# 4 MB weight transfers from expert 8 on, the last two experts summed in PSUM, and the last norm's weight spread from one row, in a single-core MoE decoder step

## The reference, cut to what matters

```python
logits = (x2d @ router_w + router_b); top_val, top_idx = lax.top_k(logits, 4); gate = softmax(top_val)
# for each of 32 experts e, on the tokens that chose it:
u = xblk @ w_up[e] + b_up[e]                   # w_up[e]: 1024 x 2048, 8 MB
glu, lin = jnp.split(u, 2, axis=-1)            # clamp both at 7
act = glu * sigmoid(1.702 * glu) * (lin + 1.0)
y = act @ w_down[e] + b_down[e]                # w_down[e]: 1024 x 1024, 4 MB
x = x + g2 * (sum over experts of gate * y)
y_prompt, y_sample = rms_norm(x, final_norm_g) # the last norm, one weight row of 1024
```

## Time and profile before

| | us |
|---|---|
| median of three runs | 1158.92 |
| the profiled execution's own time | 1159.39 |
| its span, first to last instruction | 1157.6 |
| TensorE busy | 1112.3 (96%) |
| VectorE busy | 411.7 (36%) |
| ScalarE busy | 191.3 (17%) |
| GpSimd busy | 20.7 (2%) |

### The profile page before, as it was taken

How to read it: one execution, slowest core, us unless ns; L and a number is a source line. 1 busy time by engine, 2 the same in 40 slices (tenths; PEclk the granted TensorE clock), 3 DMA queues, 4 the chain that set the end, 5 groups by cost and what they waited for, 6 DMA issues and landing times.

```text
span 1157.6 us, 14316 instructions
## 1 busy us (share of the span) xinstructions
PE 1112.3 (96%) x5674; PEld 497.2 (43%) x5674; DVE 411.7 (36%) x841; ACT 191.3 (17%) x387; POOL 20.7 (2%) x53
## 2 busy tenths in 40 slices
PE   7999999999999999999999998999999999999996
PEld 5777778843333333333333333333333333333332
DVE  3145644353333333333333334333333333333334
ACT  2161223321111111111111111111111111111112
POOL 0101010000000000000000000000000000000001
PEclk9999999999999999999999998999999999999998
DMA  9987986989999999999999999999999999999995
GB/s 352 411 308 257 367 274 231 415 316 400 429 412 430 429 426 427 429 428 428 429 429 429 429 429 427 428 427 427 427 430 425 428 428 429 428 429 428 428 429 199
DMA packets 43323, 460.96 MB, mean 398 GB/s; under 512 B 6965, under 2 KB 7937, under 8 KB 13673
## 3 DMA queue, kind: packets, MB, share of 16 engines
q1 hardware_dynamic: 37072, 449.66, 93.2%
q0 software_dynamic: 2688, 9.47, 2.3%
q10 hardware_dynamic: 3512, 1.14, 0.4%
HBM read 455.60 MB, written 4.65 MB: 398 GB/s over the span
## 4 chain that ended last, share of the span: by engine, by line
PE 73%; DMA 25%; DVE 1%; ACT 1%; issue 0%; SPq 0%; DVEq 0%; ACTq 0%
PE bank L1431 27%; DMA ring<-in_w_up 20%; PE bank L1486 14%; PE bank L1091 9%; PE bank L1472 5%; PE bank L1402 4%; DMA ring<-in_w_down 3%; PE bank L1314 2%; PE bank L1449 2%; DMA ring<-in_w_ada 2%; PE bank L1036 1%; PE bank L1411 1%; PE bank L1195 1%; PE bank L1460 1%; PE bank L1172 1%; PE bank L1277 1%
## 5 line engine op out<-in xcount | busy, mean ns | idle before, releaser
L1431 PE MATMUL bank<-ring,arena 128*64 128x512 f32 x2016 | 448.6, 595 | 21.2 <-DMA ring<-in_w_up 21.2
L1431 PEld LDWEIGHTS bank<-ring,arena 128*64 128x64 f32 x2016 | 139.7, 137 | 320.2 <-issue 277.0
L1486 PE MATMUL bank<-ring,arena 128*64 128x512 f32 x992 | 220.1, 595 | 1.9 <-DMA ring<-in_w_down 1.9
L1486 PEld LDWEIGHTS bank<-ring,arena 128*64 128x64 f32 x992 | 68.6, 137 | 131.8 <-issue 129.0
L1091 PE MATMUL bank<-arena,ring 128*128 128x264 f32 x448 | 105.4, 390 | 0.8 <-DVE arena L1696 0.8
L2043 DVE COPY arena<-bank 128x512 f32<-128x512 f32 x32 | 22.1, 692 | 197.9 <-PE bank L1431 197.9
L890 ACT ACTIVATE arena<-bank 128x512 f32<-128x512 f32 x32 | 19.1, 598 | 442.1 <-PE bank L1431 442.1
L1091 PEld LDWEIGHTS bank<-arena,ring 128*128 128x128 f32 x448 | 83.1, 190 | 17.9 <-issue 4.5
L2097 DVE TENSOR_TENSOR arena<-bank,arena 128x512 f32<-128x512 f32 x32 | 22.1, 692 | 189.7 <-PE bank L1486 189.7
L2092 DVE TENSOR_TENSOR arena<-arena,bank 128x512 f32<-128x512 f32 x128 | 79.1, 680 | 5.4 <-PE bank L1472 5.4
L1472 PE MATMUL bank<-arena,gpickT 64*128 64x512 f32 x248 | 78.6, 628 | 0.0
(11 more groups left out here) (335 smaller groups left out, 688.4 us busy)
## 6 DMA issues: line engine op xcount, KB each, us to landing
ring<-in_w_up SPq DMA_DIRECT2D x125, 2048.0 KB, 29.1
ring<-in_w_down SPq DMA_DIRECT2D x61, 2048.0 KB, 28.1
ring<-in_w_ada SPq DMA_DIRECT2D x24, 1024.0 KB, 9.5
ring<-in_w_in SPq DMA_DIRECT2D x14, 1024.0 KB, 12.0
ring<-in_w_o SPq DMA_DIRECT2D x4, 1024.0 KB, 8.5
arena<-in_w_up SPq DMA_DIRECT2D x5, 512.0 KB, 18.8
arena<-in_w_down SPq DMA_DIRECT2D x5, 512.0 KB, 12.8
ring<-in_state_hgrn POOLq DMA_DIRECT2D x4, 512.0 KB, 13.3
```

What stands on the lines that cost most here:

```text
L1431: last = mm(bank[64 * half:64 * half + 64, b, :], xe[:, par, k % 4, k // 4, :], src[:, 512 * half:512 * half + 512], start=(k == 0), stop= ...
L1486: last = mm(bank[64 * half:64 * half + 64, b, :], acts[:, k, :], src[:, 512 * half:512 * half + 512], start=(k == 0), stop=(k == KT - 1))
```

## The change

1. **4 MB transfers.** `w_up` and `w_down` are laid out anew before the launch, so that the rows of two neighbouring loads lie side by side for each partition (`up_blocks`, `down_blocks`): 32 KB contiguous per partition. From load 52 to load 187 (body 8 to the up weights of expert 31) SP sends two loads with one DMA of 4 MB into two neighbouring slots. It waits for the second of the two old loads in them, and TensorE waits for the first slot's semaphore alone. These are 68 transfers in place of 136. Loads before 52 keep 2 MB (their 16 KB rows now lie 32 KB apart), and so do the last four, the down weights of 30 and 31. `PEEL` is 8, since the loop's bodies must all be of one kind.
2. **Last two experts in the banks.** `sums_to_banks` puts `acc` into the four PSUM banks with four identity matmuls, and the combines of 30 and 31 add onto them there. VectorE's eight last additions go, and the final norm reads the banks.
3. **The norm's weight.** SP sends one 4 KB row in body 16. TensorE multiplies it with a row of ones into two banks, and ScalarE makes four copies from these. TensorE waits for the copies (`rows_sb` 7) before it goes on. The three DMAs at the end go.
4. **Squares.** VectorE now squares the second quarter (a copy and an operation) and the sample rows. ScalarE squares the other three quarters and no longer the sample rows.

```diff
-PEEL, UNROLL = 4, 4
+PEEL, UNROLL = 8, 4
+PAIRED_FROM = UPS + PEEL * LOADS
+PAIRED_TO = LOADS * NE - 4
+def comes_with_last(i):
+    return PAIRED_FROM <= i < PAIRED_TO and i % 2 == 1
...
+                sp.dma_start(pairs[:, slot:slot + n, :].rearrange("p s n -> p (s n)"), src.rearrange("e p n -> p (e n)")
+                             ).then_inc(sem(f"pair{slot}"), 16)
...
-                    reuse(i, q)
+                    if comes_with_last(i):
+                        continue
+                    n = 2 if comes_with_last(i + 1) else 1
+                    reuse(i + n - 1, q)
...
+                if e0 == MIDDLE_AT:
+                    sp.wait_ge(sem("down_done"), 3)
+                    sp.dma_start(fgraw, a["final_norm_g"].unsqueeze(0)).then_inc(sem("fg_in"), 16)
...
-            sp.wait_ge(sem("up_done"), NE)
-            sp.dma_start(fgrow, a["final_norm_g"].unsqueeze(0).to_broadcast([P, D])).then_inc(sem("fg_in"), 16)
...
+                for half in range(2):
+                    act.wait_ge(sem("bias_psum"), half + 6)
+                    own, b = slice(64 * half, 64 * half + 64), (4, 7)[half]
+                    act.activation(fgrow[:, 512 * half:512 * half + 512], bank[:, b, :], ACT.Copy).then_inc(sem("rows_sb"), 1)
+                    act.activation(fgs[own, :], bank[own, b, :], ACT.Copy).then_inc(sem("rows_sb"), 1)
...
-            for m in range(3):
-                square(m)
-            act.wait_ge(sem("sums_ready"), 2)
+            for m in (0, 2, 3):
+                act.wait_ge(sem("acc_psum"), NA * (NE - 1) + m + 1)
+                od.did(A(ring[:, 14, 512 * m:512 * m + 512], bank[:, LAST_BANKS[m], :], ACT.Square,
                          accum_out=sumsq[:, m:m + 1]), sem("squares_ready"))
+            act.wait_ge(sem("sums_ready"), 4)
...
+            def sums_to_banks(stop):
+                for m, ((i, half), b) in enumerate(zip(COMBINE, LAST_BANKS)):
+                    last = mm(bank[:, b, :], ident[:, :], acc[i][:, 512 * half:512 * half + 512], start=True, stop=stop)
...
+                pe.wait_ge(sem("fg_in"), 16)
+                for half in range(2):
+                    mm(bank[:, (4, 7)[half], :], ones[0:1, :], fgraw[:, 512 * half:512 * half + 512], start=True, stop=True
+                       ).then_inc(sem("bias_psum"), 1)
+                pe.wait_ge(sem("rows_sb"), 7)
...
             down(NE - 2, ld, rd)
+            sums_to_banks(False)
             down(NE - 1, ld, rd, (0,), 3, actT_last)
-            combine(NE - 2, LAST_BANKS, NE, None, NE)
+            combine(NE - 2, LAST_BANKS, NE, None, NE, start=False, stop=False)
             down(NE - 1, ld, rd, (1,), 3, actT_last)
-            pe.wait_ge(sem("acc_used"), NA * (NE - 1))
-            combine(NE - 1, LAST_BANKS, NE, None, NE, gpickT_last)
+            combine(NE - 1, LAST_BANKS, NE, None, NE, gpickT_last, start=False)
...
-            add_up(NE - 2, LAST_BANKS)
+            dve.wait_ge(sem("acc_psum"), NA * (NE - 1))
-            add_up(NE - 1, LAST_BANKS)
...
+            v.tensor_copy(ring[:, 15, 0:512], bank[:, LAST_BANKS[1], :]).then_inc(sem("sums_ready"), 1)
+            STT(ring[:, 15, 512:D], ring[:, 15, 0:512], 1.0, bank[:, LAST_BANKS[1], :], ALU.mult, ALU.mult,
+                accum_out=sumsq[:, 1:2]).then_inc(sem("sums_ready"), 1)
+            STT(junk_s, ys, 1.0, ys, ALU.mult, ALU.mult, accum_out=sumsq_s[:, 0:1]).then_inc(sem("sums_ready"), 1)
...
+def up_blocks(w):
+    return w[0].reshape(NE, 2, 2, P, 2, 2 * D).transpose(0, 1, 3, 2, 4, 5).reshape(NE, 2, P, 8 * D)
+def down_blocks(w):
+    return w[0].reshape(NE, 2, P, 4, D).transpose(0, 2, 1, 3, 4).reshape(NE, P, 8 * D)
```

More of the change, by code:

```diff
@@ L540, in body @@
                     else:
-                        load(i, e + 1 if kind == "up" else e, kind, k)
+                        load(i, e + 1 if kind == "up" else e, kind, k, n)
             load_aside(ASIDES[1], (0, 1, 2))
@@ L550, in _ @@
                 i = last_load(e, kind, k)
-                reuse(i)
-                load(i, e, kind, k)
+                if comes_with_last(i):
+                    continue
+                n = 2 if comes_with_last(i + 1) else 1
+                reuse(i + n - 1)
+                load(i, e, kind, k, n)
             i = last_load(*LAST[-1])
@@ L1417, in up @@
                     slot = loads(s)
[L1418 to L1421 removed]
+                    if rounds(s) is not None:
+                        pe.wait_ge(sem("aside_in" if slot < 0 else f"pair{slot}"), rounds(s))
                     if s == parts:
@@ L1461, in gates, with combine @@
                 last.then_inc(sem("gpick_psum"), 1)
-            def combine(n, banks, xes, sampled=None, picks=None, gT=gpickT):
+            def combine(n, banks, xes, sampled=None, picks=None, gT=gpickT, start=True, stop=True):
                 pe.wait_ge(sem("ysb_ready"), n + 1)
@@ L1478, in down @@
                     slot = loads(s)
-                    pe.wait_ge(sem("aside_in" if slot < 0 else f"pair{slot}"), rounds(s))
+                    if rounds(s) is not None:
+                        pe.wait_ge(sem("aside_in" if slot < 0 else f"pair{slot}"), rounds(s))
                     for kk in range(4):
@@ L1492, in down, with loads_into @@
                         last.then_inc(sem("weights_used"), 1)
+            def loads_into(slot, end):
+                return 16 * sum(expert_slot(m) == slot and m not in ASIDES and not comes_with_last(m) for m in range(end))
             def at_load(i, q=0):
@@ L2176, in _ @@
             with dve.If(n_over > 0):
+                for m, ((i, half), b) in enumerate(zip(COMBINE, LAST_BANKS)):
+                    dve.wait_ge(sem("acc_psum"), NA * (NE - 1) + m + 1)
+                    for part in range(2):
+                        c0 = 256 * part
+                        v.tensor_copy(acc[i][:, 512 * half + c0:512 * half + c0 + 256], bank[:, b, c0:c0 + 256]
+                                      ).then_inc(sem("acc_used"), 1)
                 with dve.Fori(0, EXTRA) as j:
@@ L2211, in _ @@
                 own = slice(512 * half, 512 * half + 512)
-                STT(ring[:, 12 + i, own], acc[i][:, own], sumsq[:, 5 + i:6 + i], fgrow[:, own], ALU.mult, ALU.mult
-                    ).then_inc(sem("y0_ready"), 1)
+                STT(ring[:, 12 + i, own], bank[:, LAST_BANKS[COMBINE.index((i, half))], :], sumsq[:, 5 + i:6 + i], fgrow[:, own],
+                    ALU.mult, ALU.mult).then_inc(sem("y0_ready"), 1)
 def ada_blocks(w):
```

77 lines of the change are left out of this document (39 added, 38 removed).

## The result

The changed kernel takes 1164.38 us (median of six runs, 1163.15 to 1166.13). The kernel before takes 1158.80 beside it (six runs, 1158.49 to 1160.07). The ratio is 1.0046, with a 95% interval of 1.0036 to 1.0056. So the change makes the kernel slower by 5.3 us. The time lies above my forecast of 1159.3 and at the very end of my range: the median is 0.08 us above the upper bound of 1164.3, and by the ratio it is 1158.92 x 1.0046 = 1164.3. The likeliest case, no change, did not come. What came is the mechanism of rival 1, larger than I had priced it.

What follows compares the result with a forecast made beforehand. The prediction took the weight stream to bound the kernel late in the run, then TensorE's tail and the end. Terms -4.9 + 0.3 + 0.2 + 5.9 - 1.1 = +0.4 us gave 1159.3 us, range 1155.5 to 1164.3.

Steps and rivals of the forecast that it cites:

- The likeliest case: Whole kernel: time between 1156.6 and 1161.2 us, counted as the same as before; chance 0.41.
- rival 1: Block at expert 16: the clock falls, slowing its down matmuls and draining the ring; +3.5 us, 1162.8; chance 0.17.
- stream: packets, instruction reads: Weight loads: 68 pairs save nine packets each at 8 ns, -4.9 us; extra instruction reads cost +0.2.
- stream: ring dry behind expert 16: Behind expert 16: the block grows 3.7 us, late slot reissues leave almost no margin, the stream just holds; +0.3 us.
- tail, T to the last combine: TensorE after the last binding landing: later start on the last pair and four identity matmuls; +5.9 us, bounds +4.2 and +7.
- T: Landing of u3, the last up-weight load of expert 31: 1121.85 us before, predicted near 1117.5.
- end, from the last combine: Norm and output: 0.8 us won on squares, last issue 1.1 us earlier; -1.1 us, bounds 0 and -1.6.
- The join: Joining of the norm's sums: 3.6 us after the last combine's start, where it was 4.45.
- Rival 2: Weight stream: 32 KB rows travel as two of 16 KB, saving 0.5 us instead of 4.9; 1163.7; chance 0.13.
- Rival 3: Weight stream: a packet costs 20 ns, saving 7.3 us more; 1152.0; chance 0.10.
- Rival 4: Weight stream: disturbed less, three losses of about 1 us fall away; 1156.3; chance 0.13.

Runs made afterwards that it cites:

- experiment 1: The changed kernel with the norm's weight sent as in the kernel before (three DMAs behind the last weights): 1160.69 us, ratio 1.0010.
- experiment 3: experiment 1 with the last two experts summed in SBUF and squared as before, 4 MB transfers to load 187: 1156.26 us, ratio 0.9972.
- experiment 2: The changed kernel with two unused full-width matmuls added ahead of the wait for the norm-weight copies at expert 16: 1164.18 us, ratio 1.0042.
- experiment 5: The changed kernel with all transfers at 2 MB: 1161.62 us, ratio 1.0015.
- experiment 7: experiment 1 with all transfers at 2 MB, keeping the banks and their squares: 1161.60 us, ratio 1.0015.
- experiment 4: experiment 1 with sums and squares in SBUF as before and 4 MB transfers only to load 183: 1156.28 us, ratio 0.9974.
- experiment 6: The kernel before with the new layout and 2 MB loads, plus only the norm's weight spread at expert 16: 1159.72 us, ratio 0.9997.
- experiment 8: experiment 3 with 4 MB transfers from load 28 to load 171 and four experts written out: 1156.43 us, ratio 0.9974.
- experiment 9: experiment 3 with 4 MB transfers from load 52 to load 171 only: 1154.69 us, ratio 0.9959.
- experiment 10: experiment 3 with every transfer at 2 MB, leaving only the layout and eight written-out experts: 1159.88 us, ratio 1.0003.

## Why the prediction was right in part and wrong in its likeliest case

The profiled execution against my sum, term by term:

| term | predicted | changed kernel | without part 3 (experiment 1) |
|---|---|---|---|
| stream: packets, instruction reads | -4.7 | -5.7 | -4.8 |
| stream: ring dry behind expert 16 | +0.3 | +5.6 | 0 |
| tail, T to the last combine | +5.9 | +6.6 | +5.7 |
| end, from the last combine | -1.1 | 0.0 | -0.1 |
| sum | +0.4 | +6.5 | +0.7 |

Rounding leaves 0.1 us in the last column. In the changed kernel the first row is what T (-0.1) leaves beside the two delays of 5.0 and 0.6 us. It also holds what single late landings add in each trace (0.3 to 1.6 us each, several in every trace), so it is known to about 1 us.

**The stream was right.** I took 8 ns a packet, 4.9 us for 68 pairs. T moved by 4.8 us with pairs alone. Rival 2 (long rows cut) fell by the 1486 packets. Rival 3 (20 ns a packet) fell with it; a pair wins some 0.07 us (2 x 4.89 before, 9.71 now), not 0.18. The Trainium skill's ceiling of 435.2 GB/s ("DMA: Bandwidth & Descriptors", "Where 436 GB/s comes from") had left 0.07 us for nine packets as well, and the trace agrees: pairs with nine packets fewer land every 9.71 us, 0.07 us sooner than two loads. Rival 4 expected fewer disturbances of the stream. They are still there in the changed kernel's trace (gaps of 10.75 and 10.22 us near 1082 and 1112), and the packets account for the whole gain.

**The step that failed is the ring at expert 16.** I wrote that the stream just holds, +0.3 us, with a margin of 0.2 and -0.3 us. What came is +5.6, of which the +0.3 itself, two pairs on, came as 0.6. The 5.0 us stand at the pair before, where I had left a margin of +0.2, and three sizes were too small for it. The block grew by 4.8 us, not 3.7: the steps at 711.41 and 720.03 also take 2.55 and 2.60 us, for 1.72 and 1.78 before. Experiment 3 shows the same slow steps without part 3, where the block is 723.31 - 707.12 = 16.2 us long, so they are not part 3's doing. The down of 16 took 2.6 us more at half clock, which I had left to rival 1. And the reissue needed more than the 2.6 us that I had read from a 512 KB load: it came 1.3 us behind the last landing and 5.0 us were lost, so a lead of 3.7 us would have been needed. Added up, less the margin: 1.1 + 2.6 + 1.1 - 0.2 = 4.6, against the 5.0 us of the hole; 0.4 us stay open. Rival 1, with a chance of 0.17, had the mechanism, the place and the sign, and +3.5 us; its price lacked the block's extra length and the longer lead. A margin of 0.2 us ought to have given it more than 0.17, since none of the sizes in it was known to 0.2 us.

Both halves are needed, as the runs show. Part 3 without pairs costs nothing (0.9997), and pairs without part 3 keep the ring full behind expert 16 (0.9972). Experiment 2 supports the clock's share in its trace: with full clock in the down, and 1.8 us more of block, 1.8 us of the hole go. It could not be shown in the median, and it does not separate the clock from the lead, which was 3.1 us in that trace instead of 3.7.

**The tail** was nearly right. Experiment 1 gives +5.7 for my +5.9: 1.9 from the pairs (experiment 3) and 3.8 from the banks, whose four identity matmuls take 3.6. The changed kernel has 0.9 more, since the two loads at 1101.79 ran 1.4 us long at a lower clock, of which 0.5 us did not show, since the last landing came 0.5 us late itself. But I wrote that the pairing makes over half of this term. It makes a third: the 4.4 us by which u3 starts later take away the two waits behind it (0.51 and 1.36 us), which left 2.5 us by my own sum.

**The end** failed in a smaller way. The join is 0.6 us earlier relative to the combine, for my 0.8, and so is SP's first output. It wins nothing, since the outputs then take 5.5 us to the end of the span and took 4.9. The traces tell which part this belongs to: all kernels with the banks and the new squares have it (5.3 to 5.6 in experiments 1, 2, 5 and 7), and none of those without them (4.9 in experiments 3, 4, 6, 8, 9 and 10). In the rows SP needs 2.2 us for the four prompt pieces, for 2.0 before; that is a third of the 0.6, and the rest stays open. I had ended my sum at the last issue and taken what follows it as given.

**The chances.** "Slower" had 0.37 and "same" 0.41, so the text was open to either. What I took for the likeliest is what came without part 3: 1.0010.

What stays open: why the clock falls a second time with part 3 and stays full with a block 3.4 us shorter. The runs show where it falls, not the rule. And why TensorE waited 2.55 us and then ran slowly at 1101.79 was not tested by itself. The hole is not needed for such a stretch: experiment 4, which has none, shows one at 921.28.

## What to carry to other kernels

A larger transfer saved a small sum each here (0.07 us a pair) and doubled the grain in which the ring is refilled: before pairing loads, find the longest stretch in which the consumer holds a slot, and subtract from the ring's lead what a large transfer needs on an empty queue beyond its bytes, with room to spare, since that was 2.4 to 3.7 us here. Price the parts of a change together where they use the same slack: part 3 was free with 2 MB loads and cost 0.36% with pairs, and the banks cost 2.4 us where a wait hid a part of them and 3.8 us where it did not. Use large transfers where the queue is long and end them before the tail; here loads 52 to 171 were worth 0.41%, and the three longer ranges 0.13 to 0.15 points less, with overlapping intervals.

## What the runs showed of the hardware

**A hole in the stream is invisible on the engine that consumes it.** At 730 to 740 us TensorE is 10.00 of 10 busy while DMA stands at 0.49. The loss reaches TensorE only later: behind the expert of the hole its waits of over 1.5 us for a pair begin again at 984.17, where those of experiment 1 begin at 922.75, and T comes at 1121.68 instead of 1116.96.

**A 4 MB load on an empty queue took 2.4 to 3.7 us beyond its bytes.** Three pairs were issued just behind the last queued landing. From issue to landing they took 13.45 us in the changed kernel (737.08), 12.77 in experiment 2 (735.42) and 12.07 in experiment 8 (345.22), for 9.71 in a full queue. So the excess is 3.7, 3.1 or 2.4 us and no constant of the size. For a load of 512 KB it is 2.6 us, which I had carried over. In the changed kernel the DMA engines also ran empty over some 3 us rather than at once: their share is 0.42 from 732 to 734 and 0.04 from 734 to 736.

**The clock.** Part 3's small-row matmuls and waits are followed by a second stretch at the 1.2 GHz level. It is in all four kernels that have part 3: the down took 9.71, 9.56 and 9.19 us in three of them, and in experiment 2 the two added matmuls took 3.63 us, in the down's stead. A lower clock also followed some of the longer waits for DMA. TensorE waited 2.55 and 2.50 us before a pair in the changed kernel and in experiment 2, and the pair behind took 8.51 and 8.78 us. Behind waits of 1.87 and 1.93 us (experiments 1, 3 and 4) it took 7.09. But the length of the wait does not decide alone, as experiments 3 and 4 show, in this order:

```profile
951.89 7.09 PE L1447 MATMUL bank<-ring,arena 128*64 128x512 f32 x32 [2.54 <-DMA ring<-in_w_up]
```
```profile
921.28 8.76 PE L1447 MATMUL bank<-ring,arena 128*64 128x512 f32 x32 [2.21 <-DMA ring<-in_w_up]
```

In the changed kernel the slow stretch at 1101.79 has this row:

```profile
1101.80:1104.80 3.00, 3.00 (x8) 0.98 (x10) 0.00 (x0) 0.00 (x0) 0.00 (x0) 0.52 0.96 415
```

Its granted clock is 0.52, the 1.2 GHz level. Pairing makes the regular waits longer (about 1.8 us, where they were 0.64 and 1.24), since one wait stands where two were before. A single late landing can do it with 2 MB loads too: in experiment 5 a wait of 2.78 us at 1074.13 is followed by 5.35 us for a load that takes 3.65.
